# Moving one modulation part out of the attention loop and issuing its value products one unit behind, in a two-layer RWKV-7 / sparse-attention trunk

## What is computed

```python
sh1, sc1, gt1, sh2, sc2, gt2 = split(silu(c) @ ada_w[layer] + ada_b[layer], 6)   # per layer
h = rms_norm(x, norm_g[layer, 0]) * (1 + sc1) + sh1
y = rwkv7_time_mix(h, ...) if layer == 0 else nsa_attention(h, w_qg, w_o, *shared)
x = x + gt1 * rms_norm(y, norm_g[layer, 1])
h = rms_norm(x, norm_g[layer, 2]) * (1 + sc2) + sh2
x = x + gt2 * rms_norm(square(relu(h @ w_up)) @ w_down, norm_g[layer, 3])
```

## Time and profile before

| | |
|---|---|
| median of 3 runs | 1070.82 us (1069.36 to 1076.25) |
| the profiled execution: its time, its span | 1069.96 us, 1068.2 us |
| mean granted TensorE clock over the span | 0.922 of 2.4 GHz |
| TensorE busy | 892.7 us (84%), 7485 instructions |
| VectorE busy | 670.6 us (63%), 717 instructions |
| ScalarE busy | 415.7 us (39%), 583 instructions |
| GpSimd busy | 159.5 us (15%), 198 instructions |
| HBM read | 166.42 MB, 157 GB/s over the span |

### The profile page before, as it was taken

How to read it: one execution, slowest core, us unless ns; L and a number is a source line. 1 busy time by engine, 2 the same in 40 slices (tenths; PEclk the granted TensorE clock), 3 DMA queues, 4 the chain that set the end, 5 groups by cost and what they waited for, 6 DMA issues and landing times.

```text
span 1068.2 us, 17565 instructions
## 1 busy us (share of the span) xinstructions
PE 892.7 (84%) x7485; PEld 758.7 (71%) x7485; DVE 670.6 (63%) x717; ACT 415.7 (39%) x583; POOL 159.5 (15%) x198
## 2 busy tenths in 40 slices
PE   2376897768788789999999999795777889999997
PEld 2254886558677556999999789783445759999986
DVE  5843477664575274999999673625445566755453
ACT  2115432123433335444444464313336474434441
POOL 8621410234324030000000031300000000000000
PEclk9688987869999989999999999978889899999998
DMA  8800433231233106699999358520220047756550
GB/s 332 273 1 1 165 113 117 79 115 37 90 121 118 64 21 218 243 370 362 383 369 378 110 165 253 162 93 2 79 79 2 1 158 243 270 197 190 175 188 40
DMA packets 71807, 170.16 MB, mean 159 GB/s; under 512 B 5401, under 2 KB 6705, under 8 KB 71730
## 3 DMA queue, kind: packets, MB, share of 16 engines
q1 hardware_dynamic: 68784, 160.75, 43.3%
q0 software_dynamic: 2384, 7.15, 2.2%
q10 hardware_dynamic: 562, 1.15, 0.3%
HBM read 166.42 MB, written 1.05 MB: 157 GB/s over the span
## 4 chain that ended last, share of the span: by engine, by line
PE 50%; DVE 31%; issue 7%; ACT 6%; DMA 3%; POOL 2%; SPq 0%; DVEq 0%; ACTq 0%; POOLq 0%
DVE wlo L1035 7%; PE ps L1634 5%; PE ps L1645 5%; PE ps L1636 5%; PE ps L1649 5%; PE ps L1647 5%; PE ps L1637 5%; DVE acc L1257 4%; PE ps L1860 3%; DVE gt L975 2%; DMA raw<-in_ada_w_dram 2%; PE ps L1462 2%; PE ps L1896 2%; ACT whi L635 2%; DVE acc L975 2%
## 5 line engine op out<-in xcount | busy, mean ns | idle before, releaser
L1035 DVE TENSOR_TENSOR wlo<-raw,whi 128x2048 fp32r<-128x2048 f32 x94 | 218.5, 2324 | 82.7 <-ACT whi L635 80.8
L635 ACT ACTIVATE whi<-raw 128x2048 fp32r<-128x2048 f32 x94 | 178.6, 1907 | 143.7 <-DMA raw<-in_mlp_down_dram 90.5
L1634 PE MATMUL ps<-ghi,whi 128*128 128x256 f32 x576 | 163.6, 284 | 3.3 <-DVE glo L1219 1.2
L1637 PE MATMUL ps<-ghi,wlo 128*128 128x256 f32 x576 | 163.0, 283 | 0.0
L1636 PE MATMUL ps<-glo,whi 128*128 128x256 f32 x576 | 163.0, 283 | 0.0
L1634 PEld LDWEIGHTS ps<-ghi,whi 128*128 128x128 f32 x576 | 110.5, 192 | 6.0 <-issue 5.6
L1636 PEld LDWEIGHTS ps<-glo,whi 128*128 128x128 f32 x576 | 110.5, 192 | 0.7 <-issue 0.2
L1637 PEld LDWEIGHTS ps<-ghi,wlo 128*128 128x128 f32 x576 | 110.5, 192 | 0.0
L1645 PE MATMUL ps<-whi,hidhi 128*128 128x512 f32 x256 | 101.3, 396 | 2.6 <-DVE wlo L1035 2.6
L1647 PE MATMUL ps<-whi,hidlo 128*128 128x512 f32 x256 | 100.5, 392 | 0.0
L1649 PE MATMUL ps<-wlo,hidhi 128*128 128x512 f32 x256 | 100.4, 392 | 0.0
(11 more groups left out here) (333 smaller groups left out, 1770.6 us busy)
## 6 DMA issues: line engine op xcount, KB each, us to landing
raw<-in_mlp_up_dram SPq DMA_DIRECT2D x32, 1024.0 KB, 5.7
raw<-in_mlp_down_dram SPq DMA_DIRECT2D x32, 1024.0 KB, 5.2
raw<-in_ada_w_dram SPq DMA_DIRECT2D x24, 1024.0 KB, 5.3
late<-in_ada_w_dram SPq DMA_DIRECT2D x24, 1024.0 KB, 9.5
late<-in_kv_ada_w_dram SPq DMA_DIRECT2D x8, 1024.0 KB, 9.4
raw<-in_kv_w_dram SPq DMA_DIRECT2D x6, 1024.0 KB, 5.2
raw<-in_rw_k_dram SPq DMA_DIRECT2D x4, 1024.0 KB, 13.2
raw<-in_rw_r_dram SPq DMA_DIRECT2D x4, 1024.0 KB, 5.1
```

What stands on the lines that cost most here:

```text
L635: sc.activation(whi[i][:, :, :], raw[i][:, :].rearrange("p (k n) -> p k n", k=4), ACT.Copy).then_inc(s_hi, 1)
L1035: st.tell(dv.tensor_tensor(wlo[i][:, :, :], raw[i][:, :].rearrange("p (k n) -> p k n", k=4), whi[i][:, :, :].bitcast(F32), ALU.subtract), ...
L1634: mm(out_, whi[b][:, k, cols], hi[:, k0 + k, :], start=(first and k == 0 and m % 2 == 0), stop=False, skip_group_check=True)
L1637: ins = mm(out_, wlo[b][:, k, cols], hi[:, k0 + k, :], start=False, stop=False, skip_group_check=True)
```

## The change

- Part 4 of layer 1 leaves the stream and becomes part 7 of eight late parts (in front of part 5). There are 36 late pieces. The first four (part 5 of layer 0) are issued behind W pieces 15 (three) and 16 (one), and VectorE takes them ahead of the norms of the output projection of layer 0. Feed-forward 0 still has 28 late pieces and feed-forward 1 four.
- The accumulators have eight rows (`acc8`), `nrow1` moves to another address, `acc_b`, `mid_half` and `ada_half` go. The columns of part 4 are made with three others (`layer_two_cols`: four in place of three), with products of 112 columns in place of 128; the sixteen TensorE rows behind the attention loop go.
- In the output projection of layer 0 the turn of block 0 stands behind the third piece of the second pass, not the second (`turn_at`).
- `weight_low(q0 + 2)` moves ahead of the copy of the gates and of the wait for the compressed hidden values.
- Unit 0 is scaled ahead of the compressed softmax; in the loop VectorE scales u+1 in front of the maxima of u+2, and TensorE issues the value products of u-1 behind the scores of u+2. Unit 0's turn has the scores of unit 2 between its two kinds of products.

```diff
-                      *((ada1, A["ada_b"][1], part) for part in (0, 1, 2, 3, 5))]
+                      *((ada1, A["ada_b"][1], part) for part in (0, 1, 2, 3, 4, 5))]
...
-        place("wo", mid_pieces + square(A["nsa_wo"][0]))
+        place("wo", square(A["nsa_wo"][0]))
         place_feed_forward(1)
-        LATE_AFTER = {marks["ff0"] + 2 + a: a for a in range(28)}
-        LATE_AFTER.update({marks["ff1"] + 4 + 2 * a: 28 + a for a in range(4)})
+        LATE_AFTER = {15: [0, 1, 2], 16: [3]}
+        LATE_AFTER.update({marks["ff0"] + 2 + a: [4 + a] for a in range(28)})
+        LATE_AFTER.update({marks["ff1"] + 4 + 2 * a: [32 + a] for a in range(4)})
...
             v.wait_ge(n_xr, 16)
+            for a in range(4):
+                ada_late(a)
             both_norms(gt[0], "gm2", "sh2", ghi, glo, 16)
...
+            weight_low(q0 + 2)
             v.wait_ge(n_gt_ps, 1)
...
-            weight_low(q0 + 2)
             weight_low(q0 + 3)
...
+            scaled(0)
             v.wait_ge(n_sc_ps, 1)
...
-            for u, (j, tb) in enumerate(UNITS):
-                v.wait_ge(n_e, u + 1)
...
+            for u in range(len(UNITS)):
+                if u + 1 < len(UNITS):
+                    scaled(u + 1)
+                if u + 2 < len(UNITS):
+                    maxima(u + 2)
                 if u:
                     o_copied(u - 1)
-                if u + 2 < len(UNITS):
-                    maxima(u + 2)
-                if 0 < u < 9:
-                    mid_half(u - 1)
                 if u > 13:
                     weight_low(q0 + u - 10)
...
-                for n, at_ in enumerate((3, 4, 6)):
-                    ada_columns(acc7[:, D * at_:D * at_ + D], 0, n)
+                for n, at_ in enumerate((3, 4, 6, 7)):
+                    ada_columns(acc8[:, D * at_:D * at_ + D], 0, n)
...
-            ada_columns(acc_b, 6, 0)
-            out_projection(q0 + 4, 2)
+            scores(1)
+            for u in range(len(UNITS)):
+                turn_probs(u, None if u else lambda: scores(2))
+                if 0 < u < len(UNITS) - 2:
+                    scores(u + 2)
+                if u:
+                    outputs(u - 1)
+            outputs(len(UNITS) - 1)
+            out_projection(q0 + 4, 2, 2)
```

More of the change, by code:

```diff
@@ L560, in _ @@
             norm_row(nrow[1], 0, 3)
[L561 to L563 removed]
+            st.do(g.memset(acc8[:, :], 0.0))
+            for n, (_, bias, part) in enumerate(late_parts[0:8]):
+                pool.dma_start(acc8[0:1, D * n:D * n + D], bias[D * part:D * part + D].unsqueeze(0)).then_inc(n_acc5, 16)
             pool.wait_ge(n_x, 4)
@@ L1234, in both_norms, with ada_late @@
                 weight_low(q + 1)
+            def ada_late(a):
+                v.wait_ge(late_in[a % LATE_RING], 16 * (a // LATE_RING + 1))
+                if a == 0:
+                    v.wait_ge(n_acc5, 16 * 8)
+                if a == 32:
+                    v.wait_ge(n_acc5, 16 * 9)
+                dst = acc8[:, D * (a // 4):D * (a // 4) + D] if a < 32 else acc_g[:, :]
+                for k in range(2):
+                    n = 2 * (a % 4) + k
+                    ins = dv.scalar_tensor_tensor(dst, late[a % LATE_RING][:, D * k:D * k + D], V["cs"][:, n:n + 1],
+                                                  dst, ALU.mult, ALU.add)
+                    st.tell(ins, T["late"]) if k else st.do(ins)
             def feed_forward(layer):
@@ L1705, in turned, with by_blocks @@
                 ins.then_inc(n_xT, 1)
-            def by_blocks(pieces, order, last, between=None):
+            def by_blocks(pieces, order, last, between=None, turn_at=2):
                 for n in order:
@@ L1716, in by_blocks @@
                 for n, (q, ch, ready, hi, lo, k0, first) in enumerate(pieces):
-                    if n == 2 and not last:
+                    if n == turn_at and not last:
                         turned(0)
@@ L1734, in out_projection @@
                 by_blocks([(q0 + 2 * ch + kh, ch, lambda kh=kh: ready(kh), ghi, glo, 4 * kh, kh == 0)
-                           for ch in range(2) for kh in range(2)], range(4), False)
+                           for ch in range(2) for kh in range(2)], range(4), False, None, turn_at)
             pe.wait_ge(n_xr, 16)
@@ L1886, in _, with blocks, turn_probs @@
             ins.then_inc(n_sc_ps, 1)
-            scores(1)
-            for u, (j, tb) in enumerate(UNITS):
-                blocks = [(e, br, kb) for e in range(2) for br in range(2) for kb in range(tb + 1)]
+            def blocks(tb):
+                return [(e, br, kb) for e in range(2) for br in range(2) for kb in range(tb + 1)]
+            def turn_probs(u, between=None):
+                j, tb = UNITS[u]
                 pe.wait_ge(n_pr, u + 1)
```

95 lines of the change are left out of this document (35 added, 60 removed).

## The result

The changed kernel took 1045.36 us (median of 4 runs, 1043.0 to 1047.06) beside 1070.09 us of the kernel before (4 runs, 1066.75 to 1076.25): ratio 0.977, 95% interval 0.974 to 0.980, so 21 to 28 us faster. The prediction was 1042.0 us, range 1031 to 1057. The profiled execution took 1046.21 us with a span of 1044.4, at a mean granted clock of 0.924 (before 0.922).

The account below looks back on a forecast made before the run. It took VectorE to bound feed-forward 0 and a circle of waits to pace the attention loop. Terms + 14.8 + 1.3 - 5.7 - 40 + 1.6 = - 28.0 took 1069.96 to 1042.0 us, range 1031 to 1057.

Parts of the forecast that it names:

- The late pieces: Ahead of block 0's norm: VectorE waits for the late fourth piece, TensorE idles and restarts at half clock; cost 14.8 us.
- lower bound of 13.0: Least cost in us given for the late pieces ahead of block 0's norm, with a landing time of 7.3 us.
- The later turn: Block 0's turn behind the third piece: costs nothing inside the wait, 2.7 us if the late piece landed at once.
- Rival C: Ahead of block 0's norm: fourth late piece comes with the other three, costing under 2 us; 1029 us, chance 0.06.
- Four columns: Ahead of block 1's scale: 64 passes, not 48, take 6.4 or 7.4 us; cost 1.3 us (0.7 to 2).
- The low part: Second half of the query projection: TensorE's 4.2 us wait and 1.5 us of lower clock go; gain 5.7 us.
- The loop: Attention loop: earlier start and a pair of units in 8.7 us; gain 40 us, ends 10 and 43.
- the circle that the prediction named: Attention loop: odd scores, maxima, four exponentials, hand-over, scaling, turn up to the next odd scores; 8.7 us for two units.
- rival A: Attention loop: only the half pieces' leaving gains, pair stays at 10.9 us; gain 26 us, 1056 us, chance 0.12.
- the 36 of its final bounds: Attention loop: lower end, in us, of the gain range 36 to 43 used for the forecast's own bounds.
- Rival B: Attention loop: clock granted at 0.50 throughout, pair about 15.2 us, loop loses 5.7 us; 1088 us, chance 0.05.
- Behind the loop: Attention's output projection: TensorE idles some 4 us and may restart at half clock for 3.1 us; cost 1.6 us (0 to 1.6).

Follow-up runs that it names:

- experiment 1: Changed kernel with the two additions of late piece 3 moved into VectorE's idle places of block 1, DMAs unchanged: 1029.3 us.
- experiment 2: Changed kernel with late piece 3 issued ahead of W piece 16 instead of behind it: 1031.6 us.
- Experiment 11: Kernel of experiment 1 with block 0's turn back ahead of the third piece and five useless products behind the loop: 1025.1 us.
- experiment 9: Changed kernel with `weight_low(q0 + 2)` put back behind `hx`: 1049.3 us.
- experiment 6: Changed kernel with one extra, unneeded VectorE addition of 1.28 us in each of units 1 to 8 of the loop: 1040.4 us.
- experiment 7: Changed kernel with two extra, unneeded VectorE additions, 2.56 us, in each of units 1 to 8 of the loop: 1050.4 us.
- experiment 12: Kernel before with only the new loop order and the early low part of q0+2, half pieces staying in the loop: 1023.1 us.
- experiment 3: Changed kernel with the old loop order on both VectorE and TensorE, without the half pieces: 1062.6 us.
- experiment 8: Kernel of experiment 3 with eight unneeded additions of 1.28 us behind the maxima in units 1 to 8: 1081.2 us.
- experiment 5: Changed kernel with the old loop order on VectorE alone, TensorE keeping the new one: 1107.6 us.

## Why the prediction was right, and where it wasn't

**1. The late pieces: +14.8, measured +14.2.** Each step stands in the rows: piece 3 issued behind the `mlp_up` piece at 411.95, additions 7.9 us later (forecast 0.4 + 8.2 behind SP's W piece), TensorE idle 11.04 us (11), the turn at half clock (1.97 us). The two terms missed in opposite directions, and that the sum comes so near is luck: `xr` came 12.0 us later and not 13.9, since SP's W piece was issued 24.9 us behind the `wlo` where piece I begins and not 26.5 as before, and the late piece took 0.3 us less; behind `xr` 2.2 us were lost and not 0.9, since both turns and what followed the second ran at half clock (from the second turn to the first up-product 6.0 us, before 4.7). The prediction's lower bound of 13.0 for this part is a slip: a landing time of 7.3 gives 13.9. Experiments 1 and 2 show that the wait for that one piece is about 10 of the 14 us. "The later turn ... is inside the wait and costs nothing" holds in this kernel and only there: with the wait gone it costs 2.6 us (experiment 1 against 11). Rival C named the right alternative, and experiment 2 is that case, at 4.5 us over the kernel before and not under 2: the eight additions are not all hidden. Of the landing time the prediction had an estimate of 6.8 us from figures that the Trainium skill ("DMA: Bandwidth & Descriptors", Anatomy of one DMA) gives for DMAs issued by GpSimd. SP issued this one, and the trace has 7.9 us from issue to addition, so the row of before was the better guide.

**2. Four columns: +1.3, measured 1.7.** The 64 passes took 7.29 us, the upper of the two times considered.

**3. The low part: -5.7, measured -5.7**, and experiment 9 gives it back. Not in the sum: piece III is 1.8 us shorter. The 32 products of the compressed scores took 7.04 us before and 4.64 after. In the nine traces that have both the low part and unit 0 scaled early they took 4.1 to 5.1 us, in the five that lack one or both 6.1 to 7.0. The clock falls in all fourteen, in the five within 1.0 us of their start and in the nine 2.2 to 3.2 us behind it. Why it falls there, and later with both edits, was not found.

**4. The loop: -40, measured -39.2; the pair 8.7, measured 8.84.** The size was right, and by the rows the circle that the prediction named is not the one that closes, though it is only 0.1 to 0.2 us shorter. The prediction's circle went through the turn and the scores on TensorE. The rows show scale (767.70), maxima (769.37), exponentials, scale (771.90), maxima (773.04), exponentials, scale (776.54): VectorE and ScalarE by turns, all of the 8.84 us, TensorE not in it. TensorE's part misses it narrowly: the odd scores end at 772.85, and their maxima start 2.50 us behind the first of them where the earlier trace rows have 2.42 with VectorE waiting. Two circles of nearly one length made the sum come out, which was luck; no run here tests the two apart. What the prediction left out is the room on VectorE beside the exponentials. Experiments 6 and 7 measured it: 1.28 us a unit fits in, 2.56 costs 9.1 us. The prediction counted the half pieces' leaving as part of the gain and did not ask whether they could stay; in the new order they can (experiment 12). The part "the order gains nothing" (rival A) falls with experiment 3: 20 us are the order's. The other 19 are the halves' in the old order, half of it work and half clock (experiment 8), which the prediction had seen as a pair of 16 against 11 us. Its least gain of 10 us, the half pieces as work alone, left the clock's half out, and the 36 of its final bounds has no working.

**Rival B, the clock.** It was granted at 1.00 in the pair shown, over idles of 0.47 us. The Trainium skill ("TensorE: Matmul & The Clock Gate", A second HAM failure mode) tells of another kernel in which short, frequent idles made it swing. By that it could have moved here; the trace disagrees for these idles. It did fall in experiment 5, to 0.72 over the two units shown, with an idle of 3.05 us in every unit.

**5. Behind the loop: +1.6, measured +2.8.** The mechanism was as told, the term too small for this trace: the lower clock lasted 5.7 us (814.10 to about 819.8), not the 3.1 of the earlier trace rows. Of the ten traces that idle 4.1 to 4.2 us there, six have it for 4.8 to 5.9 us and piece V 2.3 to 2.8 us longer than before; four (experiments 1, 6, 7, 8) have it for 3.0 to 3.6 us and piece V 1.4 to 1.7 longer, which is the prediction's term. What decides between them was not found. Experiment 11 gives all of it back.

## What to carry to other kernels

Find the circle by the rows that start with no wait in front of them, engine by engine, and not by the length of a chain that fits: here two chains of 8.7 and 8.8 us exist, and a sum alone can't tell which one holds. Read the room on each engine from its waits, and test it with extra work of known length. Before work is moved out of a loop, reorder the loop and look again at who waits for whom; work that cost 2.5 us for each half piece of 1.28 in the old order was nearly free in the new one, and its new place cost 14 us. Two engines' programs that meet at every step are one schedule: here either half of the new order alone was slower than the old one (9.5 and 49 us more loop).

## What the runs showed of the hardware

- The same eight additions of 1.28 us made the loop 20.3 us longer in one order and 1.1 us in another; 10.2 of the 20.3 are the additions themselves, and the rest goes with TensorE's clock, which was 0.79 to 0.89 in the windows of that loop (experiment 8).
- After idling 4.1 to 4.2 us TensorE came back at half clock, for 3.1 us at the second half of the query projection, and behind the loop for 3.0 to 3.6 us in four traces and 4.8 to 5.9 in six, with the same products behind the idle.
- Useless products keep the clock up, but each (a pair of instructions) costs 0.82 us at full clock; ten instructions in a gap of 4.2 us made piece V 1.4 us shorter than in the kernel that they were added to (experiment 1) and 2.8 shorter than in the changed one, sixteen made it 0.2 shorter.
- The clock fell at or in the compressed scores (32 products of 30 columns) in every trace. In the kernel before it was down from their start on, behind 4.18 us of which TensorE was busy 2.67; in the changed kernel they began at full clock behind a stretch much the same, and it fell 2.7 us into them, with TensorE never idle in those. The windows, first of the kernel before, then of the changed one:

```profile
707.00:711.18 4.18, 2.67 (x19) 1.42 (x18) 1.99 (x6) 3.44 (x9) 0.00 (x0) 0.99 0.63 191
713.00:719.00 6.00, 6.00 (x26) 5.51 (x26) 0.66 (x2) 0.00 (x0) 0.00 (x0) 0.50 0.00 0
```

```profile
725.25:727.90 2.65, 2.65 (x24) 2.65 (x24) 1.03 (x3) 0.37 (x3) 0.00 (x0) 1.00 0.26 98
728.00:730.00 2.00, 2.00 (x11) 2.00 (x11) 0.01 (x1) 0.00 (x0) 0.00 (x0) 0.50 0.00 0
```
